# Two layers of 64 experts, then a block with a context: a pair of the context's blocks moved to the entry of each expert stage, the shared w1 moved to pass 16, and the late constants loaded after the second layer's experts

## What is computed

```python
def moe_ffn(u, w_router, b_router, w1, w3, w2, ws1, ws3, ws2):      # D 1024, 64 experts, top 8, FF 256
    scores = sigmoid(u @ w_router)
    ...  # 4 of 8 groups, then the 8 best experts of each token, their weights
    routed = segment_sum(swiglu(u[tokens of e], w1[e], w3[e], w2[e]) * weight)   # every expert e
    shared = swiglu(u, ws1, ws3, ws2)
    return routed + shared

def swiglu(x, w1, w3, w2):
    return (silu(x @ w1) * (x @ w3)) @ w2

# second block, first layer: hx and hc are the normed tokens and the normed context
ux, uc = hx @ ab_w_in, hc @ ab_w_in                                 # 1024 x 7184
```

## Time and profile before

| | us |
|---|---|
| median of 3 runs | 2388.41 |
| the profiled execution's own time | 2387.24 |
| its span, first to last instruction | 2385.9 |
| TensorE busy | 2310.2 (97%) |
| expert stage of layer 0, first w1 to last scatter | 390.7 to 904.2 |
| expert stage of layer 1 | 1264.8 to 1780.0 |

### The profile page before, as it was taken

The page is one execution under the profiler, slowest core; times in us unless marked ns, Lnnn a source line. Parts: engine busy times, 40 slices in busy tenths (PEclk is TensorE's granted clock), DMA queues, the critical chain, the costliest instruction groups (busy, mean ns, idle before and its releaser), DMA issues.

```text
span 2385.9 us, 34683 instructions
## 1 busy us (share of the span) xinstructions
PE 2310.2 (97%) x14075; PEld 1653.5 (69%) x14075; DVE 814.2 (34%) x2133; ACT 569.1 (24%) x1231; POOL 136.8 (6%) x181
## 2 busy tenths in 40 slices
PE   7999999999999989999999999999989999999998
PEld 4868898666666655768896666666657777854764
DVE  0376624222211211485533222112113544421264
ACT  2234412111110112234211111111113333321264
POOL 4040000000000000100000000000000000000110
PEclk9999999999999999999999999999989999999999
DMA  9785687999999997855777999999993543141300
GB/s 339 273 294 192 225 327 279 407 418 421 418 417 417 418 415 264 288 200 186 282 309 309 416 418 418 417 420 417 418 363 101 183 145 111 71 150 53 141 1 19
DMA packets 195197, 677.44 MB, mean 284 GB/s; under 512 B 14064, under 2 KB 50136, under 8 KB 144592
## 3 DMA queue, kind: packets, MB, share of 16 engines
q1 hardware_dynamic: 188064, 658.96, 71.1%
q0 software_dynamic: 6528, 16.09, 1.9%
q10 hardware_dynamic: 432, 0.01, 0.0%
HBM read 663.47 MB, written 11.55 MB: 283 GB/s over the span
## 4 chain that ended last, share of the span: by engine, by line
PE 90%; DMA 6%; DVE 2%; ACT 2%; issue 1%; SPq 0%; DVEq 0%; ACTq 0%
PE ps L282 49%; PE ps L2192 13%; PE ps L2231 7%; DMA ring<-in_w 6%; PE ps L2250 4%; PE ps L1770 3%; PE ps L708 2%; PE ps L1220 1%; PE ps L2968 1%; PE ps L3581 1%; PE ps L1137 1%; PE ps L3746 1%; PE ps L2217 1%; PE ps L3729 1%; PE ps L3738 1%
## 5 line engine op out<-in xcount | busy, mean ns | idle before, releaser
L282 PE MATMUL ps<-hT,ring 128*128 128x256 f32 x2288 | 528.3, 387 | 3.2 <-ACT ar L1590 1.9
L282 PEld LDWEIGHTS ps<-hT,ring 128*128 128x128 f32 x2288 | 427.7, 190 | 97.8 <-issue 36.4
L2192 PE MATMUL ps<-ring,ar 128*32 128x256 f32 (+2 forms) x2768 | 332.6, 388 | 10.8 <-DMA ar<-in_w 4.8
L2192 PEld LDWEIGHTS ps<-ring,ar 128*32 128x32 f32 (+2 forms) x2768 | 203.4, 128 | 108.4 <-issue 24.2
L2192 PE MATMUL ps<-ar 128*64 128x256 f32 (+1 forms) x1040 | 185.7, 394 | 10.2 <-DMA ring<-in_w 6.1
L2231 PE MATMUL ps<-ring,ar 128*32 128x512 f32 (+1 forms) x688 | 157.4, 622 | 9.1 <-DMA ring<-in_w 6.0
L2532 DVE TENSOR_TENSOR ar<-ar,ps 128x256 f32<-128x256 f32 x50 | 21.1, 422 | 421.4 <-PE ps L2192 421.4
L2560 DVE SCALAR_TENSOR_TENSOR exact_parts<-ps,ar,exact_parts 128x512 fp32r<-128x512 f32 x100 | 75.1, 751 | 213.4 <-ACT exact_parts L2386 207.8
L2386 ACT ACTIVATE exact_parts<-ps,ar 128x512 fp32r<-128x512 f32 x100 | 68.7, 687 | 304.9 <-PE ps L2231 286.9
L282 PE MATMUL ps<-ring,ar 128*128 128x512 f32 x320 | 140.2, 595 | 0.0
L2192 PEld LDWEIGHTS ps<-ar 128*64 128x64 f32 (+1 forms) x1040 | 101.7, 127 | 42.4 <-issue 19.9
(11 more groups left out here) (459 smaller groups left out, 2771.6 us busy)
## 6 DMA issues: line engine op xcount, KB each, us to landing
ring<-in_w SPq DMA_DIRECT2D x259, 1024.0 KB, 21.1
ar<-in_w SPq DMA_DIRECT2D x98, 1024.0 KB, 20.5
ring<-in_w_mod SPq DMA_DIRECT2D x36, 2048.0 KB, 11.1
ring<-in_w_in SPq DMA_DIRECT2D x28, 2048.0 KB, 11.6
ring<-in_ab_w_in SPq DMA_DIRECT2D x47, 1024.0 KB, 11.6
cst<-in_w SPq DMA_DIRECT2D x27, 1024.0 KB, 18.4
ring<-in_w_out SPq DMA_DIRECT2D x4, 2048.0 KB, 10.4
ring<-in_ab_w_out SPq DMA_DIRECT2D x2, 4096.0 KB, 13.5
```

The source lines that it names most:

```text
L282: ins = te.matmul(o, l, r, start=(first and i == 0), stop=(last and i == len(pairs) - 1), skip_group_check=lax)
L2192: ins = te.matmul(b[cols, 0:256], K.x_b[:, kk, in_pair(p, cols)], w[r][:, kk, :], start=(kk == 0), stop=(kk == 7))
```

## The change

- `ENTRY = -1` becomes a pass of its own ahead of pass 0, and `FILL_PASSES` is now ENTRY, 4, 5, 8, 12, 15, 18. So the first pair of each layer is computed in the entry, the other sets move one place forward, and pass 21 has none. In layer 1 the first two sets change places, so that the entry gets a pair (z of heads 0 and 1).
- In `pe_moe_start` the two blocks of the pair stand where the shared w1 stood, in banks 5 and 2. ScalarE copies the first one ahead of `hx_hi` and the second one behind the lists. One turned part of the tokens moves from bank 2 to bank 5, and the rotation of banks becomes 4, 6, 7, 5.
- The shared w1 is one more load in pass 16 and is applied there, ahead of w3, from the same copy of the tokens. Its silu on ScalarE moves there too.
- The ring's unit that held the shared w1 is free for experts earlier (`THIRD` in `RING_HELD`).
- The place `cst` serves the experts of layer 1 to the end, and GpSimd loads the late constants first thing in `pool_pools`, after the expert stage's last instructions.

```diff
-FILL_PASSES = [p for p in range(2, 24) if ORDER[p] > 2]
+ENTRY = -1
+FILL_PASSES = [ENTRY] + [p for p in range(2, 20) if ORDER[p] > 2]
...
-RING_HELD = [{0: NOTHING, ..., 8: ROUTER, 9: SHARED_W1},
-             {8: NOTHING, ..., 6: ROUTER, 7: SHARED_W1}]
+RING_HELD = [{0: NOTHING, ..., 8: ROUTER, 9: THIRD},
+             {8: NOTHING, ..., 6: ROUTER, 7: THIRD}]
 def in_turn(l):
-    out = []
+    out = [(-5, -3, "fill", n) for n in FILL_AT[l][ENTRY]]
...
-        if p == SHARED_W3:
-            out += [(p + 0.5, p + 0.65, name, EXPERTS) for name in ("hs", "ws3")]
+        if p == SHARED_UP:
+            out += [(p + 0.5, p + 0.65, name, EXPERTS) for name in ("hs", "ws1", "ws3")]
...
-        if l == 1 and start >= CONSTS_PASS:
-            free.pop(("consts", 0), None)
 def pe_moe_start(K, l):
...
-    w = k_major(K.flat["ws1", l], 256)
-    b = yield from K.bank(("shared_silu", l, 1), only=2)
-    te.wait_ge(*(yield ("ring", "ws1", l)))
-    for j in range(2):
-        ins = products(te, b[:, j * 256:(j + 1) * 256], [(w[:, kk, j * P:(j + 1) * P], h[:, kk, :]) for kk in range(8)])
+    for n, bank in zip(FILL_AT[l][ENTRY], (5, 2)):
+        yield from pe_fill(K, l, n, bank)
...
-            b = yield from K.bank(("hx_lo", l, i, q), only=(0, 1, 3, 2)[2 * q + i])
+            b = yield from K.bank(("hx_lo", l, i, q), only=(0, 1, 3, 5)[2 * q + i])
-def pe_shared_w3(K, l):
+def pe_shared_up(K, l):
+    te, hs = K.te, k_major(K.flat["hs", l, EXPERTS], 256)
+    te.wait_ge(*(yield ("ring", "hs", l, EXPERTS)))
+    for name, read in (("ws1", "shared_silu"), ("ws3", "shared_g")):
+        w = k_major(K.flat[name, l, EXPERTS], 256)
+        b = yield from K.bank((read, l, 1))
+        te.wait_ge(*(yield ("ring", name, l, EXPERTS)))
+        for j in range(2):
+            ins = products(te, b[:, j * 256:(j + 1) * 256],
+                           [(w[:, kk, j * P:(j + 1) * P], hs[:, kk, :]) for kk in range(8)])
...
-    K.rot, K.turn = [4, 5, 6, 7], 0
+    K.rot, K.turn = [4, 6, 7, 5], 0
 def act_moe_start(K, l):
...
-    ac.wait_ge(*(yield ("shared_w1", l)))
-    for n, cols in enumerate(SHARED_COLS):
-        ac.activation(K.gs[n], K.ps["shared_w1", l][:, cols], ACT.Silu).then_inc(*K.act("shared_silu", l, n))
+    yield from act_fill(K, FILL_AT[l][ENTRY][0])
...
+    yield from act_fill(K, FILL_AT[l][ENTRY][1])
 def pool_experts(K, l):
...
-        if late and FILL_PASS[n] >= CONSTS_PASS:
-            yield from late_consts(K)
-            late = False
 def pool_pools(K):
+    yield from late_consts(K)
     K.gp.wait_ge(*(yield ("y_turned", 1, 7)))
```

More of the change, by code:

```diff
@@ L451, in shared_part @@
             return (lambda f: k_major(f, D, 2)), I["ws2"][l].rearrange("(j p) n -> p j n", j=2)
[L452 removed]
+        return (lambda f: f[:, 0:UNIT]), K.h_kept[l] if name == "hs" else I[name][l].rearrange("(p k) f -> p (k f)", k=8)
     def experts(l):
@@ L1955, in pe_moe_start @@
     yield from pe_selected(K, l, 0)
-def pe_shared_w3(K, l):
-    te, hs, w = K.te, k_major(K.flat["hs", l, EXPERTS], 256), k_major(K.flat["ws3", l, EXPERTS], 256)
-    b = yield from K.bank(("shared_g", l, 1))
+def pe_shared_up(K, l):
+    te, hs = K.te, k_major(K.flat["hs", l, EXPERTS], 256)
     te.wait_ge(*(yield ("ring", "hs", l, EXPERTS)))
[L1963 to L1967, removed]
+    for name, read in (("ws1", "shared_silu"), ("ws3", "shared_g")):
[5 more added lines that the diff above has]
+                           [(w[:, kk, j * P:(j + 1) * P], hs[:, kk, :]) for kk in range(8)])
+        ins.then_inc(*K.pe("shared_ps", name, l, ps=b))
         K.pe.also("used", name, l, EXPERTS)
+    K.pe.also("used", "hs", l, EXPERTS)
 def pe_shared_down(K, l):
@@ L2266, in fill_weights, with pe_fill @@
     return [halves[kk // 4][:, kk % 4, at:at + 256] for kk in range(8)]
-def pe_fill(K, l, n):
+def pe_fill(K, l, n, only=None):
     te, (name, _) = K.te, FILL[n]
     w, fills = fill_weights(K, l, n), FILL_AT[l][FILL_PASS[n]]
-    b = yield from K.bank(("ctx_part", n))
+    b = yield from K.bank(("ctx_part", n), only=only)
     if n == fills[0]:
@@ L2333, in pe_experts @@
         yield from pe_turn(K, l, p)
-        if p == SHARED_W3:
-            yield from pe_shared_w3(K, l)
+        if p == SHARED_UP:
+            yield from pe_shared_up(K, l)
         if p == SHARED_DOWN:
@@ L2373, in act_experts @@
         late = len(PASS[p]) == 4 and p % 2 == 1 and p + 1 < PASSES
+        if p == SHARED_UP:
+            ac.wait_ge(*(yield ("shared_ps", "ws1", l)))
+            for n, cols in enumerate(SHARED_COLS):
+                ac.activation(K.gs[n], K.ps["shared_ps", "ws1", l][:, cols], ACT.Silu).then_inc(*K.act("shared_silu", l, n))
         fills = FILL_AT[l].get(p, [])
@@ L2543, in dve_experts @@
             yield from dve_slots(K, l, n)
-        if p == SHARED_W3:
-            ve.wait_ge(*(yield ("shared_w3", l)))
+        if p == SHARED_UP:
+            ve.wait_ge(*(yield ("shared_silu", l, 1)))
+            ve.wait_ge(*(yield ("shared_ps", "ws3", l)))
             for n, cols in enumerate(SHARED_COLS):
-                ve.tensor_tensor(K.gs[n], K.gs[n], K.ps["shared_w3", l][:, cols], ALU.mult).then_inc(*K.dve("shared_g", l, n))
+                ve.tensor_tensor(K.gs[n], K.gs[n], K.ps["shared_ps", "ws3", l][:, cols], ALU.mult).then_inc(*K.dve("shared_g", l, n))
         if LISTING <= p < LISTING + 8:
@@ L2572, in pool_experts @@
         K.ev["hc_kept",] = (K.s_hc, 16)
-    late = l == 1
     for n in FILL_OF[l]:
-        if late and FILL_PASS[n] >= CONSTS_PASS:
-            yield from late_consts(K)
-            late = False
         gp.wait_ge(*(yield ("ctx_part", n)))
@@ L2580, in pool_experts @@
         gp.dma_start(K.ctx_parts[:, at:at + 512], K.turns[:, :]).then_inc(K.s_parts, 16)
-    if late:
-        yield from late_consts(K)
     if l == 0:
```

14 lines of the change are left out of this document (5 added, 9 removed).

## The result

The changed kernel takes 2391.82 us (median of 22 runs), the kernel before 2387.98 us (22 runs). The ratio is 1.0017 with a 95% interval of 1.0011 to 1.0023: 3.8 us slower by the medians, 2.6 to 5.5 us by the interval. The forecast was +3.8 us, a median of 2392.3. The profiled execution took 2393.14 us, its span is 2391.8, so it lies 1.3 us above its median, where the profiled one of before lies 0.7 under its own. The two traces are therefore 5.9 us apart, 2 us more than the medians.

The account below looks back on a forecast made before the run. The prediction took each expert stage to be bound by its stream of loads, TensorE outside them. A 7.3 us later start less 4.3 gave +3.0 in layer 0, +0.8 in layer 1 after constants: +3.8, median 2392.3 us, forecast's own range 2390 to 2396.

Parts of the forecast that it names:

- What bounds the stage: Both expert stages: bound by their stream of loads, at a DMA share of 1.01 and 414 and 413 GB/s.
- The start: Entry of each layer: second block uncovered, 7.12 us, plus 0.2 us for bank 5; the stream starts 7.3 us later.
- The stream: Expert stage: one load and two stores fewer, 3.8 us, plus 0.5 us for dearer pair's loads; 4.3 us shorter.
- +1.0 us: Bound on the sum: added if the pair's loads are no dearer than others.
- The constants: Layer 1: 0.918 MB leave the stream, 2.2 us less; their load after the last scatter is hidden, at 0.
- The whole: Whole kernel: 3.0 us in layer 0 and 0.8 in layer 1, +3.8 us, median 2392.3 us.
- Signs: Profile after: ranks near 388, w1 of pass 0 near 398, SyncE's load near 401.7, layer 0's last w2 near 899.3 us.
- TensorE's waits for loads in the middle of the stage: Sign in passes 14 to 18: waits for DMA shorter, while those in passes 22 to 24 get longer.
- TensorE as the bound: Rival: the entry's 7.1 us come back in the stage, in all 0 to +1 us, 2389; chance 0.16.
- the swallowed start: Rival: only bytes count, each layer gains 4.3 us and layer 1 2.2 more, 2377.6 us; chance 0.14.
- late constants: Rival: VectorE and TensorE wait for the constants, 3.1 us and more, 2395.4 up to 2400 us; chance 0.14.
- a bound of +1.5 us: Last w2 of layer 0: some +1.5 us if longer waits in passes 22 to 24 leave TensorE slow to its end.

Follow-up runs that it names:

- constants alone: The kernel before with only the late constants loaded behind the experts and their place serving layer 1's experts to the end: 2386.07 us, ratio 0.9995.
- busy alone: The kernel before with six unread products of the identity ahead of the wait for the last pass's w2: 2382.24 us, ratio 0.9976.
- the two that alter layer 1 alone: The changed kernel, in layer 1 only: 14 of 16 shared w1 products left out in pass 16, 2390.88 us; or the shared w1's load left out, 2390.5 us.
- the one load less: The changed kernel without the shared w1's load in layer 1 alone, its product using ws3's weights: 2390.5 us, ratio 1.0014.
- Two edits that changed the loads of layer 0: Changed kernel without the shared w1's load in each layer, 2401.3 us; version with one single block in each entry, place not mended, 2400.96 us.

## Why the prediction was right

**What bounds the stage.** Right. The two stages run at 412 to 414 GB/s and a share of 1.01, before and after. 6.2 us of TensorE's work out of a stage gave 0.3 and 0.9 us, three loads more per layer cost 15.2 us of 15.2 in the traces. The 358 GB/s that the Trainium skill gives as a core's share of HBM ("DMA: Bandwidth & Descriptors", section "Where 436 GB/s comes from") is passed by 15% for some 500 us on end in both stages. By it the three loads would have cost 17.6 us in the two layers together, an estimate.

**The start.** Right. 7.12 + 0.2 us were forecast, and 7.26 measured in layer 0 and 7.15 in layer 1. The parts are 6.90 and 0.35 in layer 0, so the total is closer than its terms. VectorE's 7.25 us of waiting shows that the second block was not covered, and 12.4 us of its products taken out of the two entries gave 12.5 at the end (9.4 to 15.6 by that kernel's interval).

**The stream.** This is the term that was mis-sized. 4.3 us were taken off, 3.8 for a load and two stores and 0.5 because the pair's loads seemed dearer. The 3.8 were right: 1.57 MB at the same 413 GB/s. The 0.5 were not found: layer 0's stream is 3.9 us shorter and not 4.3, and the whole stream runs at the same rate with one pair fewer. The 11 GB/s between two windows of 20 us were no price of a pair that comes back at the end. The prediction had this case among its bounds, as +1.0 us. Single traces give the entry's cost to w2 only roughly, so take those whose layer 0 is the same up to the last w2: 529.3 us (the mean of 529.44, 528.28, 529.71 and 529.63: the changed kernel, the one with the constants back in the stage and the two that alter layer 1 alone) less 525.5 (the mean of 526.08, 525.63 and 524.78: before, constants alone, busy alone) is **+3.8 us, where 3.0 were forecast**. 0.5 of the 0.8 are the price of the pair that was not found. The other 0.3 stay open: they are less than the 1.4 us by which these equal stages differ.

**The constants.** -2.2 us forecast; -2.5 by the trace of the one that moves them alone, -1.4 by the changed kernel against the one without, and -1.2 (-3.3 to +1.0) by time. Their load is hidden; it took 8.4 us and not 10.2, and landed 5 us ahead of its reader. The DMA engines were busy beside it (a share of 1.04 to 1.06 from 1785 to 1795 us), and the second block's four loads of 1 MB that SyncE issued from 1780 to 1800 us took 11.5 us as a median. The trace agrees with the Trainium skill's rule ("DMA: Bandwidth & Descriptors", section "Queues, rings and completion order"), by which an engine takes the queues in turn. For layer 1 the sum was +0.8, and +0.95 us from router to turned tokens was measured. That closeness is luck. To w2 it is +2.2: the start came 7.15 us later, and from SyncE's issue to the last w2 it took 497.24 us for 502.19, 5.0 less where 6.5 were taken off (4.3 and 2.2). The clock of w2 then gave 1.2 us back to the changed kernel (8.43 us for 9.67).

**The whole.** +3.8 us forecast, +3.8 measured by the medians and +4.1 by the ratio. The mechanism was right, and the fit to 0.1 us is luck. By the traces the entry cost some 0.8 us more in each layer than the sum said. About as much is missing from the whole again: w2 ran faster in layer 1's trace by 1.2 us, but whether it does so in the median run is not measured.

**Signs.** Ranks at 388.09 for 388, w1 of pass 0 at 398.37 for 398, SyncE's load at 402.07 for 401.7, last w2 at 900.07 for 899.3, stage of layer 1 4.7 us later for 4. One sign was wrong: TensorE's waits for loads in the middle of the stage did not get shorter, 4.8 us after for 4.1 before between 640 and 760 us. They did grow late in the stage: 12.8 us after for 8.7 before between 800 and 905 us, `issue` counted, and 7.1 for 4.6 by the waits for loads alone.

**The rivals.** TensorE as the bound and the swallowed start are refuted by the runs above, late constants by the trace, in which line 1145 is released by ScalarE and not by the load.

## What to carry to other kernels

When a stage is bound by a stream at full rate, its end is its start plus its bytes: price every edit in these two, and TensorE's work inside the stage at nothing as long as TensorE still waits for loads behind it. Ahead of such a stage, put in the shade of another engine only as much as that shade is long; what stands over costs in full even when it takes the same work out of the stage. Read a change of bytes from the bytes themselves at the mean rate of the whole stream, not from the rate of a 20 us window.

## What the runs showed that was not expected

The same w2, scatter and copies at the end of a stage take 6.7 to 9.7 us, by TensorE's clock after its last wait for a load. Where that wait was 1.5 to 1.9 us (six stages of five kernels, three of them filled) it was 6.73 or 6.74 us each time. In all other stages the wait was 1.98 to 4.6 us, and it took 8.0 to 9.7. The prediction saw the slow records in the kernel before and priced only what a longer wait might add, as a bound of +1.5 us. It did not ask what the wait already cost. It is the largest thing to be had here: six products without use, which cost nothing while the stream is the bound, gave 5.7 us, more than the whole change moved. The spread also hides small gains, as it hid most of the one load less.

The second thing is the table of places. Two edits that changed the loads of layer 0 made SyncE stand some 54 us at the router of layer 1, and both kernels ended near 2401 us where 2387 and 2385 were expected. Such a run looks like a refuted theory until SyncE's own waits are read.
